# Two of every eight rows of the modulation sums go from VectorE to ScalarE, their order among the low halves changes, and the sigmoid's table is chosen sooner

## The reference

```python
mod = silu(c) @ w_ada + b_ada                        # 1024 x 6144
sh1, sc1, gt1, sh2, sc2, gt2 = split(mod, 6)
h   = rms_norm(x, g_pre_mix) * (1 + sc1) + sh1
zin = h @ w_in                                       # 1024 x 3072
# group A: conv value, conv gate -> sigmoid gate, causal depthwise conv, layer norm, swish
# group B: q, f, i, og -> gated linear recurrence in chunks of 64
x   = x + gt1 * rms_norm(concat(A, B) @ w_out, g_post_mix)
x   = x + gt2 * rms_norm(swiglu(rms_norm(x, g_pre_ffn) * (1 + sc2) + sh2), g_post_ffn)
```

## Time and profile before

| | us |
|---|---|
| median of 3 timed runs | 1190.41 |
| lowest and highest | 1188.95, 1190.81 |
| profiled execution, its own time | 1186.35 |
| profiled execution, span of the core | 1184.6 |
| TensorE busy | 1141.7 (96%) |
| VectorE busy | 740.9 (63%) |
| ScalarE busy | 306.1 (26%) |
| GpSimd busy | 661.9 (56%) |

### The profile page before, as it was taken

The page is one execution under the profiler, slowest core; times in us unless marked ns, Lnnn a source line. Parts: engine busy times, 40 slices in busy tenths (PEclk is TensorE's granted clock), DMA queues, the critical chain, the costliest instruction groups (busy, mean ns, idle before and its releaser), DMA issues.

```text
span 1184.6 us, 13775 instructions
## 1 busy us (share of the span) xinstructions
PE 1141.7 (96%) x5528; PEld 953.0 (80%) x5528; DVE 740.9 (63%) x893; ACT 306.1 (26%) x460; POOL 661.9 (56%) x388
## 2 busy tenths in 40 slices
PE   2799999999999999999999999999999999999996
PEld 2678888888887888878888888888888888888885
DVE  5776979979988655658744444444444444444447
ACT  5455254272341624341110101010101010101014
POOL 4045434342333460315486868686877777777755
PEclk9999999999999999999999999999999999999999
DMA  9545323232310153202112020202020203020216
GB/s 331 170 130 155 102 77 91 89 89 77 102 36 26 47 206 114 89 25 66 36 36 71 30 77 22 85 20 88 18 89 18 89 19 89 19 89 18 89 40 262
DMA packets 94097, 98.52 MB, mean 83 GB/s; under 512 B 2925, under 2 KB 80978, under 8 KB 94034
## 3 DMA queue, kind: packets, MB, share of 16 engines
q1 hardware_dynamic: 92576, 93.33, 25.0%
q10 hardware_dynamic: 1458, 4.31, 0.9%
HBM read 89.25 MB, written 8.39 MB: 82 GB/s over the span
## 4 chain that ended last, share of the span: by engine, by line
PE 92%; DVE 3%; ACT 1%; SPq 1%; DMA 1%; issue 1%; ACTq 0%; DVEq 0%
PE pair L1716 31%; PE pair L1637 27%; PE pair L1529 24%; PE pair L1565 4%; PE pair L1694 1%; PE pair L1492 1%; DVE acc L959 1%; DMA x<-in_x 1%; SPq L404 1%; PE pair L1579 1%; PE pair L1560 1%; PE pair L1453 1%; PE pair L1441 1%; PE pair L1581 1%; PE pair L1574 1%
## 5 line engine op out<-in xcount | busy, mean ns | idle before, releaser
L1081 DVE SCALAR_TENSOR_TENSOR pair<-u,conv_w_col,pair 128x512 f32<-128x512 f32 x240 | 162.5, 750 | 1.2
L1393 DVE TENSOR_TENSOR yt<-yt,pair 128x1024 f32<-128x1024 f32 x80 | 97.6, 1220 | 95.2 <-PE pair L1637 95.1
L604 POOL TENSOR_TENSOR w_lo<-raw,w_hi 128x1024 fp32r<-128x1024 f32 x66 | 146.6, 2222 | 5.3
L602 POOL CAST w_hi<-raw 128x1024 fp32r<-128x1024 f32 x66 | 68.6, 1040 | 121.2 <-PE pair L1637 52.5
L525 POOL TENSOR_TENSOR w_lo<-raw,w_hi 128x1024 fp32r<-128x1024 f32 x21 | 52.4, 2499 | 104.6 <-ACT w_hi L689 104.6
L1637 PE MATMUL pair<-w_hi,u_hi 128*128 128x512 f32 x352 | 108.6, 390 | 0.3 <-DVE yt L1391 0.3
L1637 PE MATMUL pair<-w_lo,u_hi 128*128 128x512 f32 x352 | 108.4, 389 | 0.0
L1637 PE MATMUL pair<-w_hi,u_lo 128*128 128x512 f32 x352 | 108.4, 389 | 0.0
L604 POOL TENSOR_TENSOR w_lo<-sraw,w_hi 128x1024 fp32r<-128x1024 f32 x38 | 104.3, 2744 | 3.0
L602 POOL CAST w_hi<-sraw 128x1024 fp32r<-128x1024 f32 x38 | 39.5, 1039 | 117.7 <-PE pair L1637 116.0
L536 POOL TENSOR_TENSOR acc<-acc,ada 128x1024 f32<-128x1024 f32 x28 | 67.4, 2406 | 52.4 <-ACT ada L733 51.1
(11 more groups left out here) (259 smaller groups left out, 2583.5 us busy)
## 6 DMA issues: line engine op xcount, KB each, us to landing
ada<-in_w_ada SPq DMA_DIRECT2D x48, 512.0 KB, 3.9
raw<-in_w_ffn_in SPq DMA_DIRECT2D x44, 512.0 KB, 3.9
raw<-in_w_in SPq DMA_DIRECT2D x24, 512.0 KB, 3.9
raw<-in_w_ffn_out SPq DMA_DIRECT2D x22, 512.0 KB, 3.4
x<-in_x SPq DMA_DIRECT2D x8, 512.0 KB, 8.4
raw<-in_w_out SPq DMA_DIRECT2D x8, 512.0 KB, 3.4
x<-in_x SPq DMA_DIRECT2D x4, 1024.0 KB, 8.1
out<-x ACTq DMA_DIRECT2D x8, 512.0 KB, 2.6
```

The lines of the kernel that those rows point to most:

```text
L602: me.done(pool.tensor_copy(w_hi[:, g % WS, cols], src[:, cols]))
L604: pool.tensor_tensor(w_lo[:, g % WS, cols], src[:, cols], w_hi[:, g % WS, cols], ALU.subtract).then_inc(w_split, 1)
L1081: i_ = dve.scalar_tensor_tensor(out=dst, in0=src, scalar=w, in1=dst, op0=ALU.mult, op1=ALU.add)
L1393: dve.tensor_tensor(yt[:, i, :], yt[:, i, :], pair[2 + n % 2][:, :], ALU.add).then_inc(y_added, 1)
```

## The change

ScalarE makes the products of rows 0 and 1 of blocks 1, 2 and 3, in the new `first_rows(b)`: block 1's between groups 2 and 3, block 2's after group 3, block 3's after group 6. VectorE no longer makes them and waits for both (`acc_begun`) ahead of row 2; from row 4 on it waits for its own last but one sum as before. On VectorE the rows of blocks 2 and 3 stand at other places among the low halves: rows 2 to 5 of block 2 ahead of low half 4, its last rows and addition ahead of low half 5; rows 4 and 5 of block 3 ahead of low half 8, its last rows and addition ahead of low half 9. ScalarE's Exp moves from behind group 15 to behind group 3, and the sigmoid's table is asked for right after it. Block 0 is summed by VectorE alone as before.

```diff
+            def first_rows(b):
+                act.wait_ge(ada0_loaded[2 * b], 32)
+                if b > 1:
+                    act.wait_ge(mod0_summed, 2 * b - 2)
+                for j in range(2):
+                    act.activation(acc0[:, b % 2, j, :], ada0[:, b % ADA_RING, j, :, :].rearrange("p s n -> p (s n)"),
+                                   ACT.Copy, scale=cond[:, j:j + 1]).then_inc(acc_begun, 1)
             squares(range(TT))
             for g in range(16):
                 full_and_high(g)
-            act.wait_ge(vec_ready, 2)
-            act.activation(lb_tmp[:, 1, :], lb_tmp[:, 0, :], ACT.Exp).then_inc(cond_ready, 1)
+                if g in (2, 3, 6):
+                    first_rows({2: 1, 3: 2, 6: 3}[g])
+                if g == 3:
+                    act.wait_ge(vec_ready, 2)
+                    act.activation(lb_tmp[:, 1, :], lb_tmp[:, 0, :], ACT.Exp).then_inc(cond_ready, 1)
+                    act.preload_act_table_set("sigmoid_and_others")
             act.wait_ge(vec_ready, 3)
...
                     else:
-                        me.wait(behind=1)
+                        if b and j == 2:
+                            dve.wait_ge(acc_begun, 2 * b)
+                        if b == 0 or j > 3:
+                            me.wait(behind=1)
...
             low_half(0)
             low_half(1)
-            sum_rows(1, range(2))
             low_half(2)
             sum_rows(1, range(2, 4))
             low_half(3)
             sum_rows(1, range(4, KT))
-            sum_rows(2, range(2))
             scale_shift(2)
             scale_shift(3)
-            sum_rows(2, range(2, 4))
+            sum_rows(2, range(2, 6))
             low_half(4)
-            sum_rows(2, range(4, 6))
+            sum_rows(2, range(6, KT))
             low_half(5)
-            sum_rows(2, range(6, KT))
             low_half(6)
             scale_shift(4)
+            sum_rows(3, range(2, 4))
             low_half(7)
-            sum_rows(3, range(3))
             scale_shift(5)
+            sum_rows(3, range(4, 6))
             low_half(8)
-            sum_rows(3, range(3, 6))
+            sum_rows(3, range(6, KT))
             low_half(9)
-            sum_rows(3, range(6, KT))
             low_half(10)
```

More of the change, by code:

```diff
@@ L231, in build @@
         ada0_loaded = [sem(f"ada0_loaded{i}") for i in range(KT)]
+        acc_begun = sem("acc_begun")
         acc_ready = sem("acc_ready")
```

## The result

The changed kernel took 1181.91 us in the median of 7 timed runs (1181.24 to 1184.51), the kernel before 1188.71 us in 7 runs beside it (1185.93 to 1190.81). The ratio is 0.9949, 95% interval [0.9937, 0.9961]: 6.1 us (4.6 to 7.5) faster.

A forecast was written before the change was run, and what follows sets the result against it. Three VectorE sums and one ScalarE table load, for which TensorE waits, were taken to set the stage; +0.65 +0.3 -2.0 -1.3 -1.3 gave -3.6 us, from 1190.41 to 1186.8 us, range 1185.2 to 1189.6 (8 in 10).

The forecast's parts named there:

- the last of the sum: Whole kernel: the 3.6 us gain is taken off the timed median 1190.41, 4.06 above the profiled execution, giving 1186.8 us.
- Block 1: the new wait: VectorE before rows 2 and 3 of block 1: waiting for ScalarE's two products makes the sum 0.65 us later.
- The clock: TensorE in group 3's products, moved later: part of them runs at 1.2 GHz, 0 to 0.6 us lost, 0.3 charged.
- Block 2 and block 3: VectorE's sums: low half 4 to block 2's end 2.7 us instead of 4.67; addition to addition 9.0 instead of 10.28.
- ScalarE's queue: ScalarE before group 4: waits 0.9 us for rows landing at 33.8, is done at 37.9, with 2.7 us of cover.
- The sigmoid: First gate chunk: without the table load ahead of it, the sigmoid starts 1.28 us earlier.
- A: Rival, chance 0.05: the table load comes back in front of the sigmoid; gain only 2.3 us, 1188.1 us.
- B: Rival, chance 0.13: block 1 comes later than by 0.65 through ScalarE's order or TensorE's clock; 1187.8 to 1188.8 us.
- C: Rival, chance 0.06: the stage ends 3.6 us earlier but a later stage gives it back; no change, 1190.4 us.
- D: Rival, chance 0.05: after block 1's longer wait TensorE's clock stays at 1.2 GHz through groups 4 to 8; slower, 1195.5 us.

The follow-up runs named there:

- the two parts of the change: Kernel before with only Exp and the sigmoid's table choice moved behind group 3: 1185.85 us; changed kernel with Exp and both loads back behind group 15: 1185.20 us.
- the second trace: The changed kernel run once more with nothing altered: 1183.06 us, 0.9951 of the kernel before.

## Why the prediction was wrong

**The step that failed** is the last of the sum: "I leave that difference as it is, since nothing in the stage bears on it, and take the same 3.6 off". Two things were wrong in it. First, the difference of 4.06 us hung on a median of three runs, 1190.41. Beside the changed kernel the median was 1188.71, and over all 90 runs it is 1188.54, 2.2 above the profiled execution. So 1.7 of the 4.9 us between 1186.8 and 1181.91 are scatter in the starting point and no effect of the change. Second, something in the stage did bear on the difference: TensorE's clock at 1.2 GHz behind the very waits that the change shortens, which the profiled execution had been spared.

What the runs showed in its place: a fall behind one of these waits costs 1.5 (sigmoid) or 1.6 us (block 2, block 3); keeping TensorE busy in the three takes 2.7 us off the kernel before; the two parts of the change are worth 2.6 and 3.7 us where their own steps give 1.3 and 2.3; and with the clock held up on both sides 3.4 to 4.2 us are left, the 3.6 of the sum. The two traces' 2.7 us in the stage and the count's 2.3 us of falls make 5.0, inside the measured 4.6 to 7.5 and about 1 us short of its middle. The range went wrong with the step: it had the runs' spread as noise on the result and not as a term that the change can remove. Its lower end, by its own terms (1186.8 less 0.3 for the clock and 1.9), would be 1184.6 and not 1185.2; the result lies below both.

**Block 1: the new wait.** Right: 0.63 for the 0.65 forecast. The gap on VectorE and the order in ScalarE's queue were as told.

**The clock.** The mechanism was right and the size off: 1.1 us for the 0.3 charged. The fall came earlier, near 37.3, and covered all of group 3; in the second trace, at 39.1, it cost less, for block 1's end to low half 4 took 5.50 us, 0.46 more than before. The middle between nothing and 0.6 had no upper end for a fall that comes earlier. The Trainium skill (TensorE: Matmul & The Clock Gate, The HAM clock gate) has an idle TensorE gated down to 1.2 GHz. The traces agree, with six falls behind the twelve full waits for block 2, block 3 and the sigmoid; I applied the rule to the one wait that got longer and not to the three that got shorter.

**Block 2 and block 3.** Right in their distances: 2.75 for 2.7 and 9.00 for 9.0, and TensorE's waits for the additions are 0.38 and 0.40. The clock's 0.8 us beyond the forecast stand in front of both: block 2's sum came 0.2 earlier than before, counted from the first low half, in place of 1.0.

**ScalarE's queue.** Right: the landing at 33.4 (forecast 33.8), free at 37.55 (forecast 37.9).

**The sigmoid.** Right: no load, the wait 0.61.

**Rivals.** A did not happen. B happened by its clock, 0.8 us of it, in the profiled execution. C did not: the rest is 1113.3 to 1113.4 us in every trace in which the clock does not fall between the third chunk and the end stage, nine of thirteen, of the kernel before, the changed one and variants. D did not.

**What stays open.** The fall near 358 in one trace of the changed kernel has no counterpart elsewhere, and how often each wait is followed by a fall is known from four traces each. The changed kernel's 0.48 us at the start is scatter: low0 lies between 27.4 and 28.3 in the thirteen traces, at 27.61 and 28.34 in the two of the changed kernel. That the loss of the timed runs is all clock rests on the filled waits, the correlation and the count, not on a trace of every run.

## What to carry to other kernels

Look where the profiled execution stands among the timed ones before adding a delta to the median, and take more than three of them: if it is among the fastest, something costs time in the others, and a change may take that away too. Count every wait of TensorE of about 2 us amid dense products as a chance (here 6 in 12) of 1.5 to 1.6 us more on top of its own length. Filling a wait with useless products tells the two costs apart in one run, and where the wait can't be removed it is itself worth a little: 1181.41 against 1183.06 us here, with block 1's products back on VectorE.

## What the runs showed of the hardware that was not expected

TensorE's clock can fall after the wait, when the engine is busy again: in the kernel before run again TensorE waited from 69.3 to 71.2 with 1.00 granted and had 0.51 from 72.3 to 75.5, fully busy. So its cost falls on the dense work that comes next, and the clock shown for the wait itself gives no sign of it. That the wait lets it fall is shown by filling it: no fall followed in nine such places. Whether it falls differs between executions of one program: one trace of the kernel before has a fall there, the other has none, and keeping only some of the waits busy left falls behind the others. The wait for block 1, which nobody meant to change in the kernel before, varies too: it was 1.56, 1.70, 1.87 and 1.71 us in four traces of that stage unchanged, each with a fall behind it, and 1.46 and 0.62 us in two more, with none.
